# Two adaLN units in each scan group with the condition as the stationary operand, four instead of eight on VectorE in W_out

## The reference

```
s_lat = jax.nn.silu(c)[:, None, :]
s_ctx = jax.nn.silu(c_ctx)[None, None, :]
sh1, sc1, g1, sh2, sc2, g2 = jnp.split(s_lat @ w_ada[i] + b_ada[i], 6, axis=-1)
a_lat = modulate(rmsnorm(x_lat, norm1_w[i]), sh1, sc1)
x_lat = x_lat + g1 * m_lat
f_lat = swiglu(modulate(rmsnorm(x_lat, norm2_w[i]), sh2, sc2), ...)
```

## Time and profile before

| | |
|---|---|
| three runs | 1351.91, 1353.47, 1355.84 us; median 1353.47 |
| span of the profiled execution | 1352.0 us |
| PE busy | 1195.1 us (88%) |
| DVE busy | 914.0 us (68%) |
| ACT busy | 591.0 us (44%) |
| POOL busy | 91.5 us (7%) |
| four scan groups | about 104.5 to 448 us of the span |
| W_out | about 470 to 567 us |

### The profile page before, as it was taken

The page is one execution under the profiler, slowest core; times in us unless marked ns, Lnnn a source line. Parts: engine busy times, 40 slices in busy tenths (PEclk is TensorE's granted clock), DMA queues, the critical chain, the costliest instruction groups (busy, mean ns, idle before and its releaser), DMA issues.

```text
span 1352.0 us, 20115 instructions
## 1 busy us (share of the span) xinstructions
PE 1195.1 (88%) x7100; PEld 690.1 (51%) x7100; DVE 914.0 (68%) x1419; ACT 591.0 (44%) x1023; POOL 91.5 (7%) x105
## 2 busy tenths in 40 slices
PE   5849898998989599799999999997989967799997
PEld 2424454454544344334444444444855536688886
DVE  3676767857666589898887886746347656756654
ACT  3644453744656442243333342222335534566642
POOL 0004014050040000000000000000000000000000
PEclk8778889998899799899999999998999987899998
DMA  9211111121111416625565554440321101455552
GB/s 381 99 59 63 63 63 62 35 89 62 63 63 63 155 51 230 217 112 198 186 221 191 208 194 164 159 136 32 125 94 62 62 32 65 150 190 189 207 192 97
DMA packets 24238, 171.84 MB, mean 127 GB/s; under 512 B 2688, under 2 KB 2688, under 8 KB 5504
## 3 DMA queue, kind: packets, MB, share of 16 engines
q1 hardware_dynamic: 18288, 128.23, 26.1%
q0 software_dynamic: 5184, 37.75, 7.8%
q10 hardware_dynamic: 720, 5.24, 1.0%
HBM read 170.17 MB, written 1.05 MB: 127 GB/s over the span
## 4 chain that ended last, share of the span: by engine, by line
PE 71%; DVE 16%; ACT 4%; issue 4%; DMA 2%; POOL 1%; DVEq 1%; SPq 0%; ACTq 0%; POOLq 0%
PE bank L1421 19%; PE bank L1422 18%; PE bank L1423 18%; DVE arena L944 2%; DMA arena<-wada 2%; PE bank L1747 1%; DVE arena L830 1%; PE bank L1613 1%; PE bank L1602 1%; PE bank L1761 1%; DVE wl L800 1%; PE bank L1448 1%; DVE arena L877 1%; PE bank L1734 1%; PE bank L1736 1%
## 5 line engine op out<-in xcount | busy, mean ns | idle before, releaser
L1421 PE MATMUL bank<-hh,wh 128*128 128x512 f16 (+1 forms) x1136 | 395.3, 348 | 47.6 <-ACT arena L429 28.9
L800 DVE SCALAR_TENSOR_TENSOR wl<-raw,wh 128x1024 f16<-128x1024 f32 x224 | 266.3, 1205 | 206.8 <-ACT wh L389 205.7
L1422 PE MATMUL bank<-hl,wh 128*128 128x512 f16 (+1 forms) x1136 | 394.4, 347 | 0.0
L1423 PE MATMUL bank<-hh,wl 128*128 128x512 f16 (+1 forms) x1136 | 393.8, 347 | 0.0
L389 ACT ACTIVATE wh<-raw 128x1024 f16<-128x1024 f32 x224 | 229.1, 1043 | 281.7 <-PE bank L1423 210.8
L1421 PE MATMUL bank<-arena,wh 128*128 128x512 f16 (+1 forms) x544 | 181.5, 334 | 10.9 <-DVE wl L800 3.7
L1421 PEld LDWEIGHTS bank<-hh,wh 128*128 128x128 f16 x1136 | 113.1, 100 | 151.7 <-issue 66.8
L1422 PE MATMUL bank<-arena,wh 128*128 128x512 f16 (+1 forms) x544 | 181.3, 333 | 0.0
L1423 PE MATMUL bank<-arena,wl 128*128 128x512 f16 (+1 forms) x544 | 181.3, 333 | 0.0
L830 DVE SCALAR_TENSOR_TENSOR arena<-arena,araw 128x1024 bf16<-128x1024 f32 x144 | 167.6, 1219 | 0.2
L1423 PEld LDWEIGHTS bank<-hh,wl 128*128 128x128 f16 x1136 | 112.9, 99 | 94.8 <-issue 8.0
(11 more groups left out here) (214 smaller groups left out, 1344.3 us busy)
## 6 DMA issues: line engine op xcount, KB each, us to landing
raw<-wgu SPq DMA_DIRECT2D x44, 1024.0 KB, 4.8
arena<-wadaT POOLq DMA_DIRECT2D x36, 1024.0 KB, 5.1
raw<-wdn SPq DMA_DIRECT2D x16, 896.0 KB, 4.7
raw<-wxg SPq DMA_DIRECT2D x12, 1024.0 KB, 5.0
arena<-wada SPq DMA_DIRECT2D x8, 1024.0 KB, 18.0
raw<-wz SPq DMA_DIRECT2D x8, 1024.0 KB, 4.7
raw<-wout SPq DMA_DIRECT2D x8, 1024.0 KB, 4.8
raw<-wdn SPq DMA_DIRECT2D x8, 1024.0 KB, 4.9
```

Source lines behind the costliest of these rows:

```text
L800: ve.scalar_tensor_tensor(wl[:, u.slot, a:b], raw[:, u.slot, a:b], WS, wh[:, u.slot, a:b], ALU.mult, ALU.subtract).then_inc(lo_done, 1)
L1421: pe.matmul(o, wh[:, u.slot, wsl], ahi[:, k, t0:t1], start=st, stop=False)
L1422: pe.matmul(o, wh[:, u.slot, wsl], alo[:, k, t0:t1], start=False, stop=False)
L1423: i = pe.matmul(o, wl[:, u.slot, wsl], ahi[:, k, t0:t1], start=False, stop=en)
```

## The change

Units 8 to 15 are now made in the scan, two in each group, and W_out makes four (16 to 19) on DVE in place of eight.

In the scan the condition `s2` (2 columns) is stationary and `araw` streams, 256 columns at a time, into four column tiles of bank 7, as at the start (`ada_part`, 8 matmuls a unit). Unit 1 of the pair stands in `hooks[0][3]`, unit 2 at the end of `hooks[0][7]`. ACT copies the whole bank into `ys[:, 0]` (`ada_parts`), PE turns and adds the partial rows with four matmuls (`ada_turn`, `hooks[1][3]`), and DVE adds the bias of both units at once (`ada_out`, now right after `add_state(5)`). Both weights go through `araw`: ACT issues the first load at the group's start and the second after `exps(g, 0, 2)`, when the first has been used.

```
 ADA_FIRST = 8
-ADA_PE = ADA_FIRST + NG
-ADA_OUT = 8
+ADA_PE = ADA_FIRST + 2 * NG
+ADA_OUT = 4
...
         A_PER = 5
-        A_ADA = 4
-        A_YT = [0, 1, 2, 3]
+        A_ADA = 0
+        A_YT = [1, 2, 3, 4]
...
+            def ada_parts(g):
+
+                act.wait_ge(ap_mm, g * 2 + 3)
+                act.activation(ys[:, 0, :], AB[:, :], ACT.Copy).then_inc(ap_ok, 1)
...
-                ada_load(g + ADA_FIRST, g * A_PER - 1)
+                ada_load(g * 2 + ADA_FIRST, g * 2)
...
                 exps(g, 0, 2)
+                ada_load(g * 2 + (ADA_FIRST + 1), g * 2 + 1)
                 first_states(g)
                 exps(g, 0, 3)
                 evac_pre(u, g + 1, 0, 0)
                 evac_pre(u, g + 1, 1, 1)
+                ada_parts(g)
                 cvt(u.plus(2))
...
+            ve.memset(AB[:, :], 0.0)
...
                 add_state(g, 5)
+                ada_out(g)
                 off(g, 0)
...
-                ada_out(g + ADA_FIRST, g * A_PER + A_ADA)
                 from_chunk(g, 3)
...
-                    ada_unit(i * 4 + 2 * m, 0)
+                    ada_unit(i * 2 + m, m)
                     cvt_half(u.plus(3), 0, 0, UF // 2)
-                    ada_unit(i * 4 + (2 * m + 1), 1)
...
+            def ada_part(g, b):
+
+                pe.wait_ge(araw_in, g * 32 + (16 * b + 16))
+                if b == 0:
+                    pe.wait_ge(a_free, g * A_PER + (A_ADA + 1))
+                for n in range(2):
+                    for q in range(4):
+                        k = 4 * n + q
+                        i = pe.matmul(AB[32 * q:32 * q + 2, b * UN:(b + 1) * UN], s2[:, k, :], araw[:, k * UN:(k + 1) * UN],
+                                      start=(n == 0), stop=(n == 1))
+                i.then_inc(ap_mm, 1)
+
+            def ada_turn(g):
+
+                pe.wait_ge(ap_ok, g + 1)
+                for c in range(4):
+                    i = pe.matmul(AB[:, 2 * c:2 * c + 2], ys[:, 0, c * P:(c + 1) * P], sum4, start=True, stop=True)
                 i.then_inc(a_mm, 1)
...
+                          3: lambda: ada_part(g, 0),
...
-                          7: lambda: (within(0, 0), state(2))},
+                          7: lambda: (within(0, 0), state(2), ada_part(g, 1))},
...
-                          3: lambda: state(5),
+                          3: lambda: (state(5), ada_turn(g)),
...
-                          6: lambda: within(3, 1),
-                          7: lambda: ada(g, g * A_PER + A_ADA)},
+                          6: lambda: within(3, 1)},
```

More of the change, by code:

```diff
@@ L276, in build @@
         a0_mm = sem("a0_mm")
+        ap_mm, ap_ok = sem("ap_mm"), sem("ap_ok")
         cols_ok = sem("cols_ok")
@@ L399, in cvt_on, with ada_load @@
                     cvt_half(u.plus(1), 0, 0, UF // 2)
-            def ada_load(a, last):
-                act.wait_ge(a_mm, last + 3)
+            def ada_load(a, parts):
+                act.wait_ge(ap_mm, parts + 1)
                 act.dma_start(araw[:, :], wada[a]).then_inc(araw_in, 16)
@@ L516, in last_group @@
                 z_out(u)
+                ada_parts(g)
+                act.dma_start(araw[:, :], crow).then_inc(crow_in, 16)
                 cvt(u.plus(2))
@@ L540, in last_group @@
                 cvt(u.plus(5))
-                act.wait_ge(a_mm, g * A_PER + (A_ADA + 3))
-                act.dma_start(araw[:, :], crow).then_inc(crow_in, 16)
                 act.wait_ge(gl_ok, 8)
@@ L641, in _ @@
                 silu_xbc(0, 4 + m)
+            act.wait_ge(a0_mm, 1)
             with act.Fori(0, NG - 1) as g:
@@ L814, in _, with ada_out @@
             adaf = adac[:, :, :, :].rearrange("p l c b -> p (l c) b")
[L816 to L821, removed]
+            def ada_out(g):
+                ve.wait_ge(a_mm, g * A_PER + (A_ADA + 3))
+                at_ = bass.ds(g * 4 + 2 * ADA_FIRST, 4)
+                ve.tensor_tensor(adaf[:, at_, :], AB[:, 0:8].rearrange("p (c b) -> p c b", b=2),
+                                 cc("bada")[:, at_][:, :, None].to_broadcast([P, 4, 2]), ALU.add).then_inc(a_free, 1)
             def ada_unit(k, b):
@@ L1440, in bcast @@
                 pe.matmul(OB[1][:, cs * P:T], ones, rdg[:, cs * P:T], start=True, stop=True).then_inc(c_bc, 1)
[L1442 to L1449, removed]
+            def ada_part(g, b):
[12 more added lines that the diff above has]
+                    i = pe.matmul(AB[:, 2 * c:2 * c + 2], ys[:, 0, c * P:(c + 1) * P], sum4, start=True, stop=True)
                 i.then_inc(a_mm, 1)
-            for s, n in [(unit_done, UD), (yd, 2), (a_mm, 2), (wt_mm, 2)]:
+            for s, n in [(unit_done, UD), (yd, 2), (a_mm, 2), (wt_mm, 2), (ap_mm, 1)]:
                 pe.sem_inc(s, n)
```

## The result

The changed kernel takes 1340.13 us (median of four runs, 1335.30 to 1341.54), the kernel before 1353.66 (four runs, 1351.91 to 1355.84). The medians differ by 13.5 us. The ratio is 0.9894 with an interval of 0.9876 to 0.9912, which is 14.3 us less, between 12 and 17. I had forecast 11.0 less and 1342.5. The profiled execution has a span of 1339.2 against 1352.0 before, and its own time is 1340.88.

A forecast was written before the change was run, and what follows sets the result against it. PE was taken as the bound, with 71% of the chain (DVE 16%). Terms -6.75 - 4.8 - 4.8 + 7.8 + 2.0 - 4.5 = -11.05 took 1353.5 to 1342.5 us, range 1337 to 1350.

The forecast's parts named there:

- Ends of groups 0 to 2: Scan group ends: without the 3.6 us adaLN unit PE still waits for `z_out`, gaining 2.25 us each, -6.75.
- The clock at the starts: Starts after groups 0 to 2: PE runs at full clock up to the exponents, 1.6 us each, -4.8.
- Last end: Last group's end: `from_chunk(3)` no longer queues behind `ada_out` on DVE, so unit 4 starts earlier, -4.8.
- New matmuls: Scan units 0 and 1: parts 1.1 us, turn 0.9; +7.8 for three groups, +2.0 for the last.
- some 7 us ahead: First weight load of a group: issued at the group's start, that long before its use, so no wait.
- Second load: Scan, before the second part: ACT's load lands with 0.4 to 1.4 us to spare, cost taken as 0.
- W_out: W_out: four DVE units fewer, the `wl` gap goes and the last `residual` starts with PE's end, -4.5.
- another idle stretch, of 2.12 us, is followed by 3.44 us at 1.00: PE in the scan: evidence that the full clock follows the 1.3 us idle at group starts.
- the clock that stays low: Rival at the group starts: full clock does not return, taking back 4.8 us, 1347.3; chance 0.12.
- the tiles that do not overlap: Rival for the new parts: 3.5 us each in place of 1.1, +18.5, so 1361; chance 0.07.
- The late load: Rival: second load 1.5 to 2 us late in each of three groups, +5.5, so 1348; chance 0.08.
- The parts hide better: Rival in units 0 and 1: DVE and POOL set the pace, 1.5 us free in three groups, 1338; chance 0.08.

The follow-up runs named there:

- e3_old_moved: Kernel before, its adaLN unit in the old form moved from the group's end to after state(5) in unit 1: 1354.48 us, ratio 1.0011.
- e4_short_ada: Kernel before, with 2 of the 16 matmuls of each of its four adaLN scan units: 1337.36 us, ratio 0.9878.
- e2_one_tile: Changed kernel, all matmuls of an adaLN part in one column tile in place of four: 1362.06 us, ratio 1.0056.
- after_again: Changed kernel run and traced again without edits: 1340.22 us (six runs), ratio 0.9916.
- e1_wout_twice: Changed kernel, each of the four adaLN units in W_out doing its DVE multiplications twice: 1340.57 us, ratio 0.9915.
- first pair: The first profiled executions of the kernel before and the changed kernel: spans 1352.0 and 1339.2 us.
- second pair: Second traces of the same two programs without edits, before_again and after_again: 1352.73 and 1340.22 us.
- before_again: Kernel before run and traced again without edits: single time 1354.34 us; the kernel before in that comparison 1352.73 (eleven runs).
- e5: Changed kernel, first part of each pair moved to the end of the group before, its load one group earlier: 1335.39 us, ratio 0.9876.
- e6: As e5, with `ada_turn` moved behind `from_states(0)` and `ada_out` behind the next conversion: 1339.55 us, ratio 0.9901.

## Why the prediction was right, and where it was not

- **Ends of groups 0 to 2, forecast -6.75.** From the end of unit 3's last weight matmul (0.215 us behind its start) to the next start: 3.59, 3.49, 3.65 us before and 1.42, 1.42, 1.39 now, so -6.5. Right.
- **The clock at the starts, -4.8.** 5.49, 5.57, 5.43 us became 3.92, 3.92, 4.16, so -4.5. Right, but the margin of "a few tenths" that I had found for POOL's gating in the third start was short by 0.25. That the narrow run and not the idle goes with the low clock is shown by `e3_old_moved`; one of its four runs was followed by none.
- **Last end, -4.8.** 8.95 us from the same point to unit 4's start became 4.04, so -4.9. Right. With `ada_out` moved away and the old matmuls kept (`e3_old_moved`) the idle is 3.88 too; with the matmuls short and `ada_out` left there (`e4_short_ada`), 1.8 of the 4.9 are missing.
- **New matmuls, +7.8 and +2.0.** A part costs 1.05, the turn 0.95 (1.1 and 0.9 taken). From exponents to `from_states(0)`: 25.94, 25.93, 25.94 became 29.11, 28.25, 28.26, so +7.8; last group 27.22 became 29.11, +1.9. Of the +7.8, 0.8 is the wait for the first load at 116.48. I had judged that load in time, "some 7 us ahead", and had not reckoned with the first group, where ACT issues it at 109.90, 4 us behind the start; the other groups cost 2.3 in place of 2.6, and the two errors cancel. The wait is there only where the first start was short (5.3 us): 0.79 in this trace and 0.18 in `e2_one_tile`, none in `after_again` and `e1_wout_twice`, whose first starts took 6.7 and 6.9.
- **Second load, 0.** No wait in any group. Right.
- **W_out, -4.5.** 70.40 became 65.96, -4.4, by DVE's time (`e1_wout_twice`). Right. Another 0.6 follows between these sums and the FFN's first matmul, 8.91 us before and 8.27 now; `e1_wout_twice` has 8.91 there too.

These terms sum to -10.6 against the -11.05 forecast. The span fell by 12.8. So the mechanisms that I had named were right in kind and nearly in size, and **a term was missing**, which my sum put at nothing: the clock elsewhere in the scan.

| in the scan | forecast | first pair | second pair |
|---|---|---|---|
| ends and starts of groups 0 to 2 | -11.55 | -11.0 | -11.0 |
| last end | -4.8 | -4.9 | -4.9 |
| new matmuls | +9.8 | +9.7 | +8.8 |
| the rest, without an edit | 0 | -7.1 | -6.4 |
| whole | -6.55 | -13.3 | -13.4 |

(Each figure is rounded by itself.) The -7.1 of the first pair lie in three places (together 7.2; 0.1 was lost elsewhere):

- Unit 3 behind the idle of 2.12 us: 3.2. I had read one of three such stretches, at 1.00, and drew from it that an idle of that length leaves the clock alone. The other two of the same trace read otherwise:

```profile
171.59:187.10 15.51, 15.51 (x82) 7.38 (x84) 13.20 (x19) 9.41 (x21) 0.00 (x0) 0.89 0.21 69
...
342.38:357.89 15.51, 15.51 (x82) 7.43 (x84) 13.23 (x19) 9.41 (x21) 0.00 (x0) 0.89 0.19 68
```

  In the changed kernel all three are at 1.00. The step "another idle stretch, of 2.12 us, is followed by 3.44 us at 1.00" came to a right forecast for the 1.25 us idle, but on one case of three.
- From `within(1, 0)` to unit 3, behind the wait of 4.4 us: 23.35, 22.74, 23.24 became 22.71, 21.98, 22.04, so 2.6, at mean clocks of 0.86, 0.89, 0.87 and then 0.89, 0.92, 0.92.
- The first group's start, 6.66 us to 5.27: 1.4. This is no part of the change: `after_again` has 6.69, `before_again` 6.85.

In the second pair the shares are others: 4.8 in unit 3, 1.6 in the stretch ahead of it, 0.2 in the first start. That both pairs come to 13.3 and 13.4 is in part luck. So is the forecast's nearness to the measured median: up to the scan and from the FFN on, the traced pair gave back 5.5, the second pair 1.5, and hid most of what was missing in the first.

Why the clock falls less often in the scan of the changed kernel is not settled. PE idles before unit 3 three times in each trace, for ACT's `evac_pre` (line 429), 2.12 us in most cases and up to 2.70. Unit 3 behind these idles had the clock at 0.89 or 0.90 in:

```
kernel            before  before_again  after  after_again  e1  e2  e3  e4  e5  e6
low, of 3           2          3          0         0        0   1   0   1   0   2
```

Five of six in the kernel before against none of nine in the changed kernel and `e1_wout_twice`, whose scan is the same: that is no accident of one execution. But the long narrow run is not what decides it, for `e3_old_moved` keeps the run and has none, while `e4_short_ada`, nearly without it, has one. And the program alone does not either, as the second of these stretches in the kernel before was full in one trace, and low in the next:

```profile
256.41:272.01 15.60, 15.60 (x84) 7.52 (x84) 13.24 (x19) 9.41 (x21) 0.00 (x0) 0.89 0.20 67
```

A forecast could have put a range of 0 to 1.6 us on each, nothing sharper.

The rivals: the clock that stays low is refuted by the starts at 1.00, the tiles that do not overlap by the 1.05 us of a part; `e2_one_tile` shows what that rival would have cost, 1362 where I had worked out 1361. The late load did not happen at the second load. "The parts hide better" named 1338, near the result, but for a reason that did not occur: the parts do not hide, a group still pays 2.3 us for them.

## What to carry to other kernels

When a short piece of narrow work is moved or reshaped, price three things apart: its own time, what was hidden under it (here `z_out`, about 1.4 us of each 3.6), and the clock behind it. Look at the in-order queue of the engine that picks up its result: at the last end a 0.16 us operation waited there for the narrow run, and taking it away gave 4.9 us, 3.1 of which came already when the run was made short (`e4_short_ada`). And when one stretch of a trace is taken as evidence on the clock, read all of its siblings; the trace of before held two more, and they said the opposite.

## What the runs showed of the hardware that was not expected

- 16 fp32 passes with 2 stationary and 256 moving columns take 1.04 us in four column tiles and 3.61 in one. 32 passes with 2 moving columns take 3.6 to 3.8, and behind nine of ten such runs the clock went to its lower level for about 3.3 us (`before`, `before_again`, `e3_old_moved`; the last group of the first two, where PE idles behind the run, left out). Behind the 1.04 us parts, two in a group, it did not.
- Idles of 2.1 to 2.7 us on PE at one place of the scan left the clock at 1.00 in 21 of 30 cases and were followed by low clock in 9, in the same program at the same place both ways. Each such case costs 1.5 to 1.6 us. Behind the idles of 3.7 to 4.5 us, three in each of the ten traces, it was low for a while each time (0.61 to 0.81 over the next 8 us).
- Stretches that no edit touches differ from one kernel's trace to another by up to 4.7 us (775.5 to 780.2 from the FFN on), and between two executions of one program by 3.2. In a kernel like this, where an effect of 3 to 5 us is claimed, the trace's stretches decide and not the median.
